# Late modulation of a two-block fp32 network: multiplied and summed by GpSimd along the rows, with eight short TensorE products for the sum over the partitions

## The chip, the cores and the metric

The kernel runs on one core of a Trainium2 chip. The metric is the device time of one launch in microseconds. Engines work side by side and wait for each other by semaphores: TensorE (PE, matrix products; its weight loads are PEld), VectorE (DVE), ScalarE (ACT), GpSimd (POOL) and SyncE (SP), whose queue issues nearly all loads from HBM in the order in which they are written.

## The reference, cut to what matters

Two transformer-like blocks run one behind the other on x of 256 rows by 1024, all in fp32. The first block begins with a modulation of six vectors of 1024 numbers, made from a condition vector c and, for a second input ctx of 256 rows, from c_ctx:

```python
mod_x = silu(c) @ w_mod + b_mod              # w_mod 1024 x 6144, b_mod 6144
mod_c = silu(c_ctx) @ w_mod + b_mod
sh_m, sc_m, gt_m, sh_f, sc_f, gt_f = split(mod_x, 6)
csh_m, csc_m, _, _, _, _ = split(mod_c, 6)   # only these two of c_ctx are used
hx = rms_norm(x, g_pre_mix) * (1 + sc_m) + sh_m
hc = rms_norm(ctx, g_pre_mix) * (1 + csc_m) + csh_m
qa, ka, va, qr, kr, vr, gr = split(h @ w_in)          # for hx and hc
qa = rms_norm(qa, q_norm_g)                  # per head of 64
att, ret = attention(...), retention_both_ways(...)
mix = concat(att, head_group_norm(ret) * silu(gr)) @ w_out
x = x + gt_m * rms_norm(mix, g_post_mix)
hf = rms_norm(x, g_pre_ffn) * (1 + sc_f) + sh_f
x = x + gt_f * rms_norm(swiglu(hf), g_post_ffn)
```

So sh_m and sc_m (the first third of w_mod) are needed before anything can be projected, while gt_m is needed only behind the mix, and sh_f, sc_f, gt_f only for the block's feed-forward part. The second block (two gated feed-forward parts, a chunked linear recurrence, a convolution, cross attention to a memory "mem") isn't touched, but the keys and values of its memory are computed at the very start and in the middle of the first block.

## The kernel before, in words

**Products.** Every fp32 operand is split in a high and a low part, and a product is the sum of three TensorE products: high by high, high by low, low by high (lines 1818 to 1820, `three`). Weights come in 148 units of 1 MB (128 x 2048 numbers). For each, SyncE issues the load into one of three `raw` buffers, ScalarE makes `w_hi` from it (line 641), VectorE makes `w_lo` = raw - w_hi (line 1154), and a raw buffer is free for the load after next but one when `w_lo` is made. TensorE then runs the unit's products, while the other two engines split the next one. Units 0 to 3 are the second block's memory keys (W_K). Units 4 to 14 are `w_in` (W_IN): kr 4, 5; vr 6, 7; ka and va together 8; qa 9, 10; qr 11, 12; gr 13, 14. Units 15 to 18 are `w_out`; then come value units, and from unit 21 on the feed-forward stream. The order of the work on each engine is written out by hand in one function for each engine, with a "bank plan" that says which of TensorE's eight result banks each stage takes and who must have read it before.

**The modulation.** `w_mod` is cut in 24 blocks of 128 x 2048: block m has rows 128·(m mod 8) and columns 2048·(m div 8). `mod_unit(m)` (lines 1907 to 1926) issues four products, one for each 512 columns, with `silu_c` as the stationary operand: 32 columns wide, of which two hold the numbers of c and c_ctx and the others are zeros. The trace records each of the four as two. Their results lie side by side in one bank, `mod_row`. Eight blocks fill one row of 2048 numbers; ScalarE copies it out (`mod_row_out`), four transposes (`mod_T`, line 1933) turn it to columns, and VectorE adds `b_mod` (`mod_columns`, line 1276). Blocks 0 to 7 (sh_m, sc_m) run in the first 32 us between the memory products. Blocks 8 to 23, the late ones, are loaded as 12 "own" loads of 1 MB into two buffers (`memV` and `qrn_qan`, both not needed yet for what they are named after) and 4 in the raw ring between the units. They run on TensorE in six places: 2 behind the transposes of ctx, 3 behind kr, 3 behind unit 6, 3 behind unit 7, 3 behind unit 8 (ka, va) and 2 behind the transposes of krT. `mod_T(1)` stands behind unit 8, `mod_T(2)` behind unit 10.

**What stands around.** At the six places other engines do something for TensorE's next step: behind the ctx transposes ScalarE and VectorE turn them to `hcT_hi` and `hcT_lo` (lines 706, 1204, 1213); behind kr ScalarE copies the four kr banks out (line 719), of which vr takes one; before `states()`, which forms the retention states of ctx, VectorE takes the mean from vr (lines 1336 to 1338). qa is normalised per head: ScalarE copies it to `staged` (line 719), VectorE squares it (line 1394) and sums it (line 1395), ScalarE takes the root (line 813), VectorE the reciprocal (line 1406), and the rotated result is transposed by TensorE ahead of gr (line 1903). The mix's gain is two matrices with a gain on the diagonal, made by VectorE (`gain_diagonal`, line 1435).

**The start.** TensorE first runs six products on whatever lies in memory to raise its clock (line 1989), then transposes mem. ScalarE makes `memT_hi`, VectorE `memT_lo` (line 1240): quarters 0 and 1, then `w_lo` of unit 0, then quarters 2 and 3, then `w_lo` of unit 1. The products of `memT_lo` wait for each quarter.

## Time and profile before

| what | value |
|---|---|
| time, median of 3 runs | 1015.99 us (1015.83 to 1016.72) |
| time of the profiled execution | 1016.42 us |
| its span in the trace | 1014.6 us, so 1.8 us lie outside it |
| granted TensorE clock, mean | 0.998 |
| TensorE busy | 996.7 us, 98% |
| VectorE, ScalarE, GpSimd busy | 585.7, 494.9, 0.2 us |
| read from HBM | 186.61 MB |

The span is the time from the first to the last instruction that the profiler recorded on the core. An engine counts as busy only in instructions that compute. In the chain of waits each step leads back to what released it, so a step there is time that sets the end. In a timeline, the bracket at the end of a row is how long the engine had been idle before it and which instruction ended that.

### The profile page before, as it was taken

Reading aid. Unit: us, or ns where it says so; the run is one execution under the profiler, and the core shown is the slowest. Engines: PE = TensorE matmul, PEld = TensorE weight load, DVE = VectorE, ACT = ScalarE, POOL = GpSimd, SP = SyncE. Lnnn points to the kernel's source line nnn. Section 1 sums busy time; section 2 is a strip of 40 time slices with the busy share of each in tenths; the row PEclk is TensorE's granted clock in tenths of the full one; section 3 lists DMA queues with packets and bytes.
Section 4 is the critical chain, followed back from the end, with each engine's and each line's share of the span. In section 5 each row is a group of like instructions: output and inputs, shape, how many; then the busy total and the mean of one; then the engine's idle time right before and its main releaser. Section 6 shows DMA issues by size and latency. Waiting matters only on the chain.

```text
span 1014.6 us, 13254 instructions
## 1 busy us (share of the span) xinstructions
PE 996.7 (98%) x5168; PEld 811.4 (80%) x5168; DVE 585.7 (58%) x662; ACT 494.9 (49%) x601; POOL 0.2 (0%) x4
## 2 busy tenths in 40 slices
PE   7999999999999999999999999999999999999997
PEld 5877776778888888888888887888888878888885
DVE  5274769667555554565555665557774465555543
ACT  6473337646543443464534534663546554445432
POOL 0000000000000000000000000000000000000000
PEclk9999999999999999999999999999999999999999
DMA  9967653123655545474545465534244245555441
GB/s 371 419 272 295 276 217 125 44 109 129 219 200 176 202 167 207 166 259 171 202 165 186 166 229 177 199 125 140 109 166 166 78 148 190 201 178 201 166 166 42
DMA packets 26686, 188.32 MB, mean 186 GB/s; under 512 B 2960, under 2 KB 3216, under 8 KB 4112
## 3 DMA queue, kind: packets, MB, share of 16 engines
q1 hardware_dynamic: 26064, 185.24, 49.9%
q10 hardware_dynamic: 576, 2.43, 0.6%
...
HBM read 186.61 MB, written 1.05 MB: 185 GB/s over the span
## 4 chain that ended last, share of the span: by engine, by line
PE 93%; DVE 3%; ACT 2%; issue 1%; DMA 0%; ACTq 0%; DVEq 0%
PE bank L1818 24%; PE bank L1820 24%; PE bank L1819 24%; PE bank L2026 2%; PE bank L1862 2%; PE bank L1846 2%; PE bank L1854 2%; PE bank L1924 2%; PE bank L2292 1%; PE bank L1903 1%; PE bank L2390 1%; PE bank L2217 1%; PE bank L2168 1%; PE bank L1989 1%; PE bank L2093 1%
## 5 line engine op out<-in xcount | busy, mean ns | idle before, releaser
L1154 DVE TENSOR_TENSOR w_lo<-raw,w_hi 128x2048 fp32r<-128x2048 f32 x148 | 338.6, 2290 | 265.0 <-ACT w_hi L641 264.9
L641 ACT ACTIVATE w_hi<-raw 128x2048 fp32r<-128x2048 f32 x148 | 283.7, 1918 | 267.2 <-PE bank L1820 217.1
L1818 PE MATMUL bank<-w_hi,hT_hi 128*128 128x512 f32 (+1 forms) x760 | 299.8, 395 | 0.7 <-DVE mod L1276 0.7
L1820 PE MATMUL bank<-w_hi,hT_lo 128*128 128x512 f32 (+1 forms) x760 | 294.9, 388 | 0.0
L1819 PE MATMUL bank<-w_lo,hT_hi 128*128 128x512 f32 (+1 forms) x760 | 294.3, 387 | 0.0
L1818 PEld LDWEIGHTS bank<-w_hi,hT_hi 128*128 128x128 f32 x760 | 142.8, 188 | 33.8 <-issue 4.9
L1820 PEld LDWEIGHTS bank<-w_hi,hT_lo 128*128 128x128 f32 x760 | 142.7, 188 | 29.9
L1819 PEld LDWEIGHTS bank<-w_lo,hT_hi 128*128 128x128 f32 x760 | 142.9, 188 | 27.8 <-issue 0.2
L1818 PE MATMUL bank<-w_hi,gT_hi 128*128 128x512 f32 x264 | 103.4, 392 | 0.0
L1820 PE MATMUL bank<-w_hi,gT_lo 128*128 128x512 f32 x264 | 102.8, 389 | 0.0
L1819 PE MATMUL bank<-w_lo,gT_hi 128*128 128x512 f32 x264 | 102.7, 389 | 0.0
L1820 PEld LDWEIGHTS bank<-w_hi,gT_lo 128*128 128x128 f32 x264 | 49.5, 188 | 10.4
L1819 PEld LDWEIGHTS bank<-w_lo,gT_hi 128*128 128x128 f32 x264 | 49.6, 188 | 10.1
L1818 PEld LDWEIGHTS bank<-w_hi,gT_hi 128*128 128x128 f32 x264 | 49.6, 188 | 10.1
L916 ACT ACTIVATE arena<-bank,rstd 128x256 f32<-128x256 f32 x44 | 18.4, 470 | 63.5 <-PE bank L1820 63.5
L1570 DVE SCALAR_TENSOR_TENSOR arena<-bank,rstd,arena 128x256 f32<-128x256 f32 x44 | 19.2, 478 | 30.8 <-ACT arena L916 30.8
L1576 DVE TENSOR_TENSOR gT_lo<-bank,gT_hi 128x512 f32 (+1 forms) x33 | 22.7, 689 | 3.2
L1846 PE MATMUL bank<-w_hi,hT_hi 128*128 128x512 f32 x88 | 22.3, 395 | 2.2 <-DVE x_res L1558 0.8
L719 ACT ACTIVATE arena<-bank 128x512 f32<-128x512 f32 (+1 forms) x18 | 8.6, 552 | 32.3 <-PE bank L1820 28.8
L916 ACT ACTIVATE arena<-bank 128x256 f32<-128x256 f32 x22 | 7.2, 381 | 31.7 <-PE bank L1820 31.7
L1862 PE MATMUL bank<-w_lo,hT_hi 128*128 128x512 f32 x88 | 22.0, 392 | 0.2 <-DVE w_lo L1154 0.2
L1854 PE MATMUL bank<-w_hi,hT_lo 128*128 128x512 f32 x88 | 22.1, 393 | 0.0
...
## 6 DMA issues: line engine op xcount, KB each, us to landing
raw<-in_weights SPq DMA_DIRECT2D x152, 1024.0 KB, 4.7
arena<-in_first_mods SPq DMA_DIRECT2D x8, 1024.0 KB, 14.2
memV<-in_own_mods SPq DMA_DIRECT2D x6, 1024.0 KB, 4.8
arena<-in_own_mods SPq DMA_DIRECT2D x6, 1024.0 KB, 6.9
...
memV<-in_mem SPq DMA_DIRECT2D x1, 1024.0 KB, 5.9
x_res<-in_x SPq DMA_DIRECT2D x1, 1024.0 KB, 17.6
arena<-in_ctx SPq DMA_DIRECT2D x1, 1024.0 KB, 15.2
```

The source lines that it names most:

```text
L641: act.activation(w_hi[:, v_slot, :], raw[:, u_slot, :], ACT.Copy).then_inc(hi_ready, 1)
L916: act.activation(gate[:, c % 3, tb, :], bank[(c % 3) * 2 + tb][:, 0:256], ACT.Silu, scale=rstd[:, tb:tb + 1] if f else 1.0)\
L1154: ins = dve.tensor_tensor(w_lo[:, v_slot, n], raw[:, u_slot, n], w_hi[:, v_slot, n].bitcast(F32), ALU.subtract)
L1576: dve.tensor_tensor(gT_lo[:, s, :], bank[6][:, :].rearrange("p (a t) -> p a t", t=T), gT_hi[:, s, :].bitcast(F32), ALU.subtract).then_inc( ...
L1818: pe.matmul(out, hi, rhi, start=start, stop=False)
L1819: pe.matmul(out, hi, rlo, start=False, stop=False)
L1820: return pe.matmul(out, lo, rhi, start=False, stop=stop)
L1846: pe.matmul(out[:, :], hT_hi[:, 2 * q + e, tb * P:(tb + 1) * P], weights(w_hi, q, e), start=(first and q == quarters[0] and e == 0), stop= ...
L1854: pe.matmul(out[:, :], hT_lo[:, 2 * q + e, tb * P:(tb + 1) * P], weights(w_hi, q, e), start=False, stop=False)
L1862: ins = pe.matmul(out[:, :], hT_hi[:, 2 * q + e, tb * P:(tb + 1) * P], weights(w_lo, q, e), start=False, stop=(last and q == quarters[1] a ...
L1924: ins = pe.matmul(b[32 * j:32 * j + 32, :], silu_c[:, k, :], w[:, 512 * j:512 * j + 512], start=(k == 0), stop=(k == MOD_K - 1))
L2026: ins = pe.matmul(out[:, :], (lo if x_low else hi)[:, 4 * half + e, tb * P:(tb + 1) * P], w[:, v % RING, e * 512:(e + 1) * 512], start=(st ...
```

## The change

**GpSimd.** The late two thirds of `w_mod` come as 32 steps of 128 x 1024 numbers (512 KB): four parts of 1024 columns by eight blocks of rows. GpSimd multiplies each by its column of silu(c), one number for each partition, and adds it to a sum in `memV` (`mod_sum`). Of 32 steps 4 are a multiplication alone and 28 a multiplication and an addition. Only c is computed, not c_ctx. Steps land in turn in two halves of `qrn_qan`; the load of a step waits until the step two before is summed, and it waits in SyncE's queue, so that the loads of the units behind it wait too. Two to four steps stand behind each of the units 6 to 17.

**TensorE.** `mod_sums(part)` adds a part over the partitions: two products with a stationary operand of ones, 32 columns wide, by 512 columns each. Parts 0 and 1 stand behind units 7 and 11, parts 2 and 3 inside the mix, behind the retention's rows. The sixteen late `mod_unit` are gone. `mod_T(1)` stands behind unit 12, `mod_T(2)` in the mix. Two of the six starting products are gone.

**VectorE and ScalarE.** ScalarE squares qa, straight from the bank, and VectorE only sums. `mod_columns` and the gains move behind, to where the mix needs them. All four quarters of `memT_lo` are made before the first `w_lo`. Normalised qa takes the buffer `ret_p`, since its old place holds the late steps, and the wait for the late modulation's end (`mod_used`) is gone from VectorE.

```diff
-STREAM = [("w", v) for v in range(W_IN + 2)]
-OWN_MODS = {}
-VISITS = {W_IN + 2: 2, W_IN + 3: 3, W_IN + 4: 3, W_IN + 5: 3, W_IN + 6: 3, W_IN + 7: 2}
 W_REG = W_OUT + 2
 while (N_W - W_REG) % RING:
     W_REG += 1
-_m = MOD_K
-for _v in range(W_IN + 2, W_REG):
-    STREAM.append(("w", _v))
-    for _n in range(VISITS.get(_v, 0)):
-        if _n == 2:
-            STREAM.append(("mod", _m))
-        else:
-            OWN_MODS[_m] = (_v, _n)
-        _m += 1
-assert _m == N_MOD
-STREAM += [("w", v) for v in range(W_REG, N_W)]
-HEAD_UNITS = W_REG + N_MOD - MOD_K - len(OWN_MODS)
+STREAM = [("w", v) for v in range(N_W)]
+HEAD_UNITS = W_REG
 RAW_AT = {unit: u for u, unit in enumerate(STREAM)}
-
-
-def mods_behind(v):
-
-    own = [m for m, (at, _) in OWN_MODS.items() if at == v]
-    kind, n = STREAM[RAW_AT[("w", v)] + 1]
-    return own + ([n] if kind == "mod" else [])
+LATE = {v: 2 if W_IN + 2 < v < W_IN + 6 or v == W_OUT else 1 for v in range(W_IN + 2, W_REG)}
+LATE_STEPS = 2 * (N_MOD - MOD_K)
+assert 2 * sum(LATE.values()) >= LATE_STEPS
...
+    plan.streamed(("mod_row", 2), 0)
+    plan.signalled(("modT", 2), 2)
...
+        qan = ret_p
...
-        own_mods = [memV[:].rearrange("p b d -> p (b d)"), qrn_qan]
+        mod_sum = memV[:].rearrange("p b d -> p (b d)")
+        late_mod = [qrn_qan[:, e * 1024:(e + 1) * 1024] for e in range(2)]
...
+            late = [0]
+
+            def late_in(step):
+                if step >= 2:
+                    sp.wait_ge(sem("mod_step"), step - 1)
+                else:
+                    sp.wait_ge(mod_used, MOD_K)
+                sp.dma_start(late_mod[step % 2], io["late_mods"][step]).then_inc(sem(f"late_loaded{step % 2}"), 16)
...
-                kind, v = STREAM[u]
-                if kind == "w" and v in VISITS:
-                    for n, (m, (at, slot)) in enumerate(OWN_MODS.items()):
-                        if at == v:
-                            sp.wait_ge(mod_used, mods_behind(v)[0])
-                            sp.dma_start(own_mods[slot], io["own_mods"][n]).then_inc(sem(f"own_mod_loaded{slot}"), 16)
+                for _ in range(2 * LATE.get(u, 0)):
+                    if late[0] < LATE_STEPS:
+                        late_in(late[0])
+                        late[0] += 1
...
+        @block.gpsimd
+        def _(pool):
+            pool.wait_ge(sem("silu_c"), 1)
+            filled(pool, ("memT", 3))
+            for step in range(LATE_STEPS):
+                part, k = step // MOD_K, step % MOD_K
+                total = mod_sum[:, part % 2 * 1024:(part % 2 + 1) * 1024]
+                pool.wait_ge(sem(f"late_loaded{step % 2}"), 16 * (step // 2 + 1))
+                if k == 0:
+                    if part >= 2:
+                        pool.wait_ge(sem("mod_summed"), part - 1)
+                    pool.tensor_scalar(total, late_mod[step % 2], silu_c[:, k, 0:1], None, ALU.mult).then_inc(sem("mod_step"), 1)
+                else:
+                    pool.tensor_scalar(late_mod[step % 2], late_mod[step % 2], silu_c[:, k, 0:1], None, ALU.mult)\
+                        .then_inc(sem("mod_scaled"), 1)
+                    pool.wait_ge(sem("mod_scaled"), step - part)
+                    pool.wait_ge(sem("mod_step"), step)
+                    pool.tensor_tensor(total, late_mod[step % 2], total, ALU.add).then_inc(sem("mod_step"), 1)
...
-            mod_row_out(1)
...
-            mod_row_out(2)
             used(W_IN + 6)
             act.wait_ge(sem("kr_done"), 1)
+            act.wait_ge(sem("rope_done"), 4)
             for tb in range(TB):
+                act.activation((rope_a, rope_b)[tb], bank_of(("qa", tb))[:, :], ACT.Square).then_inc(sem("qa_squared"), 1)
                 copy_out(("qa", tb), staged[:, tb, :])
...
             act.activation(kaT[:, :], b[:, :], ACT.Copy).then_inc(read_sem(("kaT", 0)), 1)
+            mod_row_out(1)
...
+            mod_row_out(2)
...
-            split_T("memT", col("mem_norm"), hi=memT_hi, lo=memT_lo, qs=[0, 1])
-            low_to(W_K + 1)
-            split_T("memT", col("mem_norm"), hi=memT_hi, lo=memT_lo, qs=[2, 3])
+            split_T("memT", col("mem_norm"), hi=memT_hi, lo=memT_lo)
             low_to(W_K + 2)
...
+            for tb in range(TB):
+                dve.wait_ge(sem("qa_squared"), tb + 1)
+                ins = dve.reduce_sum(head_ss[:, tb * 8:tb * 8 + 8], heads((rope_a, rope_b)[tb]), AX.X)
+            ins.then_inc(sem("qa_ss"), 1)
             read_out(dve, ("qa", 1))
-            for tb in range(TB):
-                chain(dve.tensor_tensor(rope_a, staged[:, tb, :], staged[:, tb, :], ALU.mult))
-                ins = dve.reduce_sum(head_ss[:, tb * 8:tb * 8 + 8], heads(rope_a), AX.X)
-                if tb == 0:
-                    chain(ins)
-            ins.then_inc(sem("qa_ss"), 1)
             low_to(W_IN + 10)
-            mod_columns(2)
-            dve.tensor_tensor(gain_col[:, 0, :], mod[:, 16:24, 0], col("g_post_mix"), ALU.mult)
-            dve.tensor_scalar(a_ffn[:, :], mod[:, 32:40, 0], 1.0, None, ALU.add)
-            chain(dve.tensor_tensor(gain_col[:, 1, :], mod[:, 40:48, 0], col("g_post_ffn"), ALU.mult))
-            dve.tensor_tensor(a_ffn[:, :], a_ffn[:, :], col("g_pre_ffn"), ALU.mult).then_inc(sem("ffn_cols"), 1)
             dve.wait_ge(sem("qa_rms"), 1)
             chain(dve.reciprocal(head_rstd[:, :], head_rms[:, :]))
             for tb in range(TB):
                 ins = dve.tensor_tensor(heads(staged[:, tb, :]), heads(staged[:, tb, :]),
                                         heads_bc(head_rstd[:, tb * 8:tb * 8 + 8], HEADS, HD), ALU.mult)
             chain(ins)
-            dve.wait_ge(mod_used, N_MOD)
...
+            mod_columns(1)
+            dve.tensor_tensor(gain_col[:, 0, :], mod[:, 16:24, 0], col("g_post_mix"), ALU.mult).then_inc(sem("gain_col"), 1)
...
+            dve.wait_ge(sem("gain_col"), 1)
+            dve.wait_ge(sem("mod_step"), LATE_STEPS)
+            gain_diagonal(0)
...
-            for g in range(2):
-                gain_diagonal(g)
+            mod_columns(2)
+            dve.tensor_scalar(a_ffn[:, :], mod[:, 32:40, 0], 1.0, None, ALU.add)
+            chain(dve.tensor_tensor(gain_col[:, 1, :], mod[:, 40:48, 0], col("g_post_ffn"), ALU.mult))
+            dve.tensor_tensor(a_ffn[:, :], a_ffn[:, :], col("g_pre_ffn"), ALU.mult).then_inc(sem("ffn_cols"), 1)
+            gain_diagonal(1)
...
+            def mod_sums(part):
+
+                g = 1 + part // 2
+                pe.wait_ge(sem("mod_step"), MOD_K * (part + 1))
+                b = free(pe, ("mod_row", g)) if part % 2 == 0 else bank_of(("mod_row", g))
+                for e in range(2):
+                    j = part % 2 * 2 + e
+                    ins = pe.matmul(b[32 * j:32 * j + 32, :], ones[:, 0:32], mod_sum[:, 512 * j:512 * j + 512], start=True, stop=True)
+                ins.then_inc(sem("mod_summed"), 1)
...
-            for _ in range(6):
+            for _ in range(4):
...
-            for m in mods_behind(W_IN + 2):
-                mod_unit(m)
...
-                    if j < 6:
-                        for m in mods_behind(W_IN + j + 2):
-                            mod_unit(m)
-                    if j == 6:
-                        mod_T(2)
+                    if j in (3, 7):
+                        mod_sums(j // 4)
+                    if j == 8:
+                        mod_T(1)
...
+            def rows_and_sums():
+                retained_rows()
+                for part in (2, 3):
+                    mod_sums(part)
+
+            mix_out(0, 0, {1: rows_and_sums})
+            mix_out(0, 1, {0: lambda: mod_T(2)})
```

The first place in the order is TensorE's, from the last transposes of ctx to the first product of unit 6; a row here is a group of like instructions. Before:

```order
L1941 MATMUL bank<-fixed,arena 128x128 x12
L1924 MATMUL bank<-memV,silu_c 32x512 x4
L1924 MATMUL bank<-arena,silu_c 32x512 x4
L2026 MATMUL bank<-w_hi,hcT_hi 128x512 x8
L1941 MATMUL bank<-fixed,arena 128x128 x4
L2026 MATMUL bank<-w_hi,hcT_lo 128x512 x8
L2026 MATMUL bank<-w_lo,hcT_hi 128x512 x8
L2026 MATMUL bank<-w_hi,hcT_hi 128x512 x8
L2026 MATMUL bank<-w_hi,hcT_lo 128x512 x8
L2026 MATMUL bank<-w_lo,hcT_hi 128x512 x8
L1924 MATMUL bank<-memV,silu_c 32x512 x4
L1924 MATMUL bank<-arena,silu_c 32x512 x4
```

After:

```order
L1949 MATMUL bank<-fixed,arena 128x128 x12
L2034 MATMUL bank<-w_hi,hcT_hi 128x512 x8
L1949 MATMUL bank<-fixed,arena 128x128 x4
L2034 MATMUL bank<-w_hi,hcT_lo 128x512 x8
L2034 MATMUL bank<-w_lo,hcT_hi 128x512 x8
L2034 MATMUL bank<-w_hi,hcT_hi 128x512 x8
L2034 MATMUL bank<-w_hi,hcT_lo 128x512 x8
L2034 MATMUL bank<-w_lo,hcT_hi 128x512 x8
```

The two blocks ahead of the products of `hcT_hi` (line 2026 before, 2034 after) and the ones behind them are gone: these products now follow the transposes at once, and unit 6 the products of kr.

The second place is SyncE's queue of loads, from unit 6 on. Before:

```order
L574 DMA raw<-in_weights 128x2048
L609 DMA memV<-in_own_mods 128x2048
L609 DMA arena<-in_own_mods 128x2048
L611 DMA arena<-in_const 128x772
L574 DMA raw<-in_weights 128x2048
L609 DMA memV<-in_own_mods 128x2048
L609 DMA arena<-in_own_mods 128x2048
L574 DMA raw<-in_weights 128x2048 x2
L609 DMA memV<-in_own_mods 128x2048
```

After:

```order
L555 DMA raw<-in_weights 128x2048
L569 DMA arena<-in_late_mods 128x1024 x2
L599 DMA arena<-in_const 128x772
L555 DMA raw<-in_weights 128x2048
L569 DMA arena<-in_late_mods 128x1024 x4
L555 DMA raw<-in_weights 128x2048
L569 DMA arena<-in_late_mods 128x1024 x4
L555 DMA raw<-in_weights 128x2048
L569 DMA arena<-in_late_mods 128x1024 x4
```

Where one or two blocks of 1 MB stood behind a unit's load, there are two or four of 512 KB, each behind a wait for GpSimd, which the load of the next unit stands behind as well.

The third place is VectorE's queue where qa is normalised, between the making of `w_lo` of two units. Before:

```order
L1154 TENSOR_TENSOR w_lo<-raw,w_hi 128x2048
L1394 TENSOR_TENSOR arena<-arena 128x512
L1395 TENSOR_REDUCE head_ss<-arena 128x8
L1394 TENSOR_TENSOR arena<-arena 128x512
L1395 TENSOR_REDUCE head_ss<-arena 128x8
L1154 TENSOR_TENSOR w_lo<-raw,w_hi 128x2048
L1276 TENSOR_TENSOR mod<-bank,cols 128x32
L1401 TENSOR_TENSOR gain_col<-mod,cols 128x8
L1402 TENSOR_SCALAR a_ffn<-mod 128x8
L1403 TENSOR_TENSOR gain_col<-mod,cols 128x8
L1404 TENSOR_TENSOR a_ffn<-a_ffn,cols 128x8
```

After:

```order
L1165 TENSOR_TENSOR w_lo<-raw,w_hi 128x2048
L1402 TENSOR_REDUCE head_ss<-arena 128x8 x2
L1165 TENSOR_TENSOR w_lo<-raw,w_hi 128x2048
L1407 RECIPROCAL head_rstd<-head_rms 128x16
L1409 TENSOR_TENSOR arena<-arena,head_rstd 128x512 x2
```

The two squarings of 128 x 512 (line 1394) left the queue, and so did the five small instructions of the last modulation row between `w_lo` and the reciprocal (line 1406 before, 1407 after).

## Rows read from the trace of the kernel before

**Rows 1.** The page: busy time by engine.

```profile
PE 996.7 (98%) x5168; PEld 811.4 (80%) x5168; DVE 585.7 (58%) x662; ACT 494.9 (49%) x601; POOL 0.2 (0%) x4
```

**Rows 2.** Waits of TensorE, 12 to 225 us: in total, times, longest.

```profile
PE bank L1903 <- ACT arena L719: 1.2, 1, 1.2
PE bank L1967 <- DVE memT_lo L1240: 0.8, 1, 0.8
PE bank L1818 <- DVE mod L1276: 0.7, 1, 0.7
```

**Rows 3.** Windows with line 1924 alone: length, TensorE busy, weight loads busy, clock, DMA.

```profile
70.00:80.00 10.00, 2.78 (x24) 0.68 (x24) 1.00 0.64 251
...
sum 52.00, PE 14.98 PEld 3.54; mean PE 2.50 PEld 0.59
```

**Rows 4.** Chain that ended last, 60 to 78 us: start us, us, what.

```profile
62.05 1.85 PE bank L1924 x16
...
75.51 2.71 PE bank L1924 x24
```

**Rows 5.** Timeline of TensorE at five places: start us, us, line, operation, idle before.

```profile
33.45 0.36 PE L1818 MATMUL bank<-memT_hi,w_hi 128*128 128x256 f32 x1
...
117.44 0.60 PE L1933 MATMUL bank<-fixed,mod_row 128*128 128x128 f32 x4
...
121.46 0.50 PE L1818 MATMUL bank<-w_hi,hT_hi 128*128 128x512 f32 x1 [0.71 <-DVE mod L1276]
...
127.17 1.03 PE L2058 MATMUL bank<-arena 128*64 128x64 f32 x27
...
211.37 3.76 PE L2263 MATMUL bank<-arena,fixed 128*128 128x512 f32 x8
```

**Rows 6.** Timeline of ScalarE at six places.

```profile
24.41 1.15 ACT L697 ACTIVATE xn<-x_res,rstd 128x1024 f32<-128x1024 f32 x1 [0.23 <-DVE rstd L1180]
...
61.22 1.93 ACT L706 ACTIVATE hcT_hi<-bank,mod,a_mix 128x256 fp32r<-128x256 f32 x4 [1.44 <-PE bank L1941]
...
75.55 2.06 ACT L719 ACTIVATE arena<-bank 128x512 f32<-128x512 f32 x4 [3.46 <-PE bank L2026]
...
105.14 1.94 ACT L641 ACTIVATE w_hi<-raw 128x2048 fp32r<-128x2048 f32 x1
...
138.84 1.09 ACT L719 ACTIVATE arena<-bank 128x512 f32<-128x512 f32 x2 [4.90 <-PE bank L1820]
...
160.74 1.92 ACT L641 ACTIVATE w_hi<-raw 128x2048 fp32r<-128x2048 f32 x1
```

**Rows 7.** Timeline of VectorE at six places.

```profile
24.41 0.76 DVE L1184 TENSOR_SCALAR xn<-x_res,rstd 128x1024 f32<-128x1024 f32 x1
...
30.57 2.29 DVE L1154 TENSOR_TENSOR w_lo<-raw,w_hi 128x2048 fp32r<-128x2048 f32 x1 [5.40 <-ACT w_hi L641]
...
62.27 1.91 DVE L1204 TENSOR_SCALAR shifted_T<-bank,a_mix,mod 128x256 f32<-128x256 f32 x4 [3.10 <-ACT hcT_hi L706]
...
121.22 0.18 DVE L1276 TENSOR_TENSOR mod<-bank,cols 128x32 f32<-128x32 f32 x1
...
139.96 0.69 DVE L1394 TENSOR_TENSOR arena<-arena 128x512 f32<-128x512 f32 x1 [5.16 <-ACT arena L719]
...
145.59 0.24 DVE L1406 RECIPROCAL head_rstd<-head_rms 128x16 f32<-128x16 f32 x1
```

**Rows 8.** Lines of 205 to 215 us: busy us, mean ns of one.

```profile
L1435 DVE TENSOR_TENSOR arena<-fixed,gain_col 128x1024 f32<-128x1024 f32 x2 | 2.4, 1216 | 0.0
```

**Rows 9.** Windows: length, then PE, PEld, DVE, ACT, POOL busy, clock, DMA share, GB/s.

```profile
10.00:50.00 40.00, 39.17 (x301) 30.40 (x300) 16.81 (x21) 19.45 (x26) 0.00 (x0) 1.00 1.01 422
50.00:200.00 150.00, 147.80 (x1066) 110.06 (x1065) 106.78 (x200) 82.26 (x137) 0.00 (x0) 1.00 0.53 206
```

**Rows 10.** The queue of the loads, its issue near 46 us: start us, us.

```profile
46.27 0.33 SPq L609 DMA_DIRECT2D memV<-in_own_mods  x1
```

**Rows 11.** The page, DMA issues: KB each, us from issue to landing.

```profile
raw<-in_weights SPq DMA_DIRECT2D x152, 1024.0 KB, 4.7
```

More of the change, by code:

```diff
@@ L428, in two_blocks_kernel @@
         qrn_qan = carve(at, UNIT)
-        qrn = carve(at, TB, 512); at += 1024
-        qan = carve(at, TB, 512); at += 1024
+        gain_diag = [carve(at + g * 1024, 1024) for g in range(2)]; at += 1024
+        at += 1024
         k_fb = carve(at, 2, TB, 512)
@@ L1363, in _ @@
                 centre_values(tile)
-            mod_columns(1)
             read_out(dve, ("kava", 3))
@@ L1909, in mod_unit @@
                 g, k = m // MOD_K, m % MOD_K
-                if g == 0:
-                    pe.wait_ge(sem(f"mod_loaded{m}"), 16)
-                    w = first_mod[m % len(first_mod)]
-                elif m in OWN_MODS:
-                    slot = OWN_MODS[m][1]
-                    loads = sum(s == slot and n <= m for n, (_, s) in OWN_MODS.items())
-                    pe.wait_ge(sem(f"own_mod_loaded{slot}"), 16 * loads)
-                    w = own_mods[slot]
-                else:
-                    u = RAW_AT[("mod", m)]
-                    pe.wait_ge(raw_ready[u % RING], 16 * (u // RING + 1))
-                    w = raw[:, u % RING, :]
+                pe.wait_ge(sem(f"mod_loaded{m}"), 16)
+                w = first_mod[m % len(first_mod)]
                 b = free(pe, ("mod_row", g)) if k == 0 else bank_of(("mod_row", g))
@@ L2606, in lay_out @@
         "weights": np.stack([units[kind][n] for kind, n in STREAM]),
-        "first_mods": np.stack(mods[:MOD_K]), "own_mods": np.stack([mods[m] for m in OWN_MODS]),
+        "first_mods": np.stack(mods[:MOD_K]), "late_mods": np.stack([f("w_mod")[0][k * P:(k + 1) * P, c:c + 1024] for c in range(MOD_K * 256, N_MOD * 256, 1024)
+                               for k in range(MOD_K)]),
         "cols": np.concatenate([small[name] for name in COLS], axis=1),
```

22 lines of the change are left out of this document (6 added, 16 removed).

## Prediction

> **What bounds the kernel now.** I read the busy times first: TensorE works 996.7 us of a span of 1014.6, VectorE 585.7, ScalarE 494.9, GpSimd nothing [rows 1]. So the time is TensorE's work plus some 18 us in which it stands. The list of its waits up to 225 us comes next, since the change ends there: 1.2 us at the transposes of qa, 0.8 us at the low parts of mem, 0.7 us for the bank that VectorE's `mod_columns` reads [rows 2]. They are small, so what counts is work taken from TensorE, and whether other engines still keep up with it once it is gone. Then the windows with line 1924 alone: the sixteen late blocks stand in six places, and together they are busy 14.98 us [rows 3]. Last I looked at the chain there: it runs through them, 1.85 us for two blocks and 2.71 us for three [rows 4], so they lie on the path that sets the end.
>
> **TensorE: what goes.** Two places of two blocks and four of three: 2 x 1.85 + 4 x 2.71 = 14.5 us off (the 14.98 count each stretch's last modelled end as well). The wait of 0.71 us ahead of 121.46 [rows 5] goes with the move of the modulation's bank: 0.7 us off. `mod_T(1)` takes 117.44 to 117.96, 0.5 us [rows 5]. It moves behind unit 12, into the 1.2 us that TensorE waits there for ScalarE: 0.5 us off. `mod_T(2)` costs as much in the mix as it did: 0.
>
> **TensorE: what comes.** Four `mod_sums` of two products, side by side in column groups like the four of a block. A block is 2.71 / 3 = 0.90 us. If the four of a block run beside each other, two take as long as four; if they share a width, half. A full-width fp32 product by 512 columns takes 3.76 / 4 = 0.94 us (four products, recorded as eight) [rows 5], 1.9 us for two in sequence. So a part costs between 0.45 and 1.9 us; I take 0.9, the row of the same shape, thus 3.6 us in all (1.8 to 7.5).
>
> **The start.** Two starting products less and the low parts made without a `w_lo` between them: the wait of 0.8 us [rows 2] should go. But the memory products can't run ahead of the data. VectorE's `w_lo` that ends at 30.57 + 2.29 = 32.86 is used at 33.45 [rows 5, 7], 0.6 us later, and the loads have the queue full from 10 to 50 us (share 1.01, 422 GB/s) [rows 9], so `w_hi`, which that `w_lo` waits for, can't be earlier. I take 0.6 us off, between 0 and 0.9.
>
> **Covers that go.** A removed block also hid something. (1) Behind the ctx transposes: ScalarE's `hcT_hi` starts at 61.22, before TensorE is done with them at 62.05, and the first of its four pieces takes 1.93 / 4 = 0.5 us. TensorE needs it at once now, where it had 1.85 us: 0.5 us on (0 to 1.0). VectorE's `hcT_lo` has the high products and four transposes ahead of it, so nothing there. (2) Behind kr ScalarE copies four banks from 75.55 on, 2.06 / 4 = 0.5 us each, and vr takes one of them [rows 6]. Three blocks covered that. Now TensorE waits for the first copy and its semaphore: 0.7 us on (0.5 to 1.2). (3) `states()` needs the four centred vr. VectorE is done with them at 121.22 [rows 7], and TensorE reaches `states()` at 127.17 [rows 5], 5.95 us later. Counted from the end of unit 7, from where both go on, VectorE keeps its time and TensorE loses 2 x 2.71 for the six blocks, 0.52 for `mod_T(1)` and 0.71 for the wait, and gains one sum of 0.9: 5.75 us. That leaves a margin of 0.2 us, and a copy or a `w_lo` that comes in another order uses it up: 0.4 us on (0 to 1.2).
>
> **qa.** Squaring by ScalarE is 2 x 0.55 us there and 2 x 0.7 us off VectorE. The rms waited for the second sum. VectorE squares and sums from 139.96 to 142.8 and comes to the reciprocal only at 145.59 [rows 7], behind a `w_lo` and five small instructions. These go and the `w_lo` starts with ScalarE's later `w_hi`: 138.84 + 4 x 0.55 + 1.92 gives 142.96, and 2.29 more 145.25, 0.3 us earlier than 145.59. What follows is the wait of 1.2 us, which ends on ScalarE's copy of qr, not on qa [rows 2]. So the squares are worth 0 (up to 0.3 off). The two gain matrices, 1.2 us each [rows 8], and the columns go to where TensorE has a unit of gr ahead of it: 0 (0 to 1.0 on).
>
> **Sum.** -14.5 + 3.6 - 0.7 - 0.5 - 0.6 + 0.5 + 0.7 + 0.4 = -11.1 us. The profiled execution took 1016.42 us (1014.6 of span, 1.8 around it): 1005.3. It stood 0.4 us above the median of the three runs; for such a median I say 1005.1, between that and the sum less 0.4. With every term at its better end I get -14.5 + 1.8 - 1.2 - 0.9 + 0.5 - 0.3 = -14.6, with each at its worse -14.5 + 7.5 - 1.2 + 1.0 + 1.2 + 1.2 + 1.0 = -3.8; the terms don't err together, so this case's own range is 1002.5 to 1010.
>
> **GpSimd's step.** All this holds only if GpSimd keeps pace, and no row shows it computing. Bound it by others on 128 x 1024: a multiplication takes VectorE 0.76 us and ScalarE 1.15 us [rows 6, 7]; an addition of two operands takes VectorE 1.22 us [rows 8], and 2.29 us for twice the elements [rows 7], which I take as the slow end. A step is 2.0 to 3.4 us. I take 3.4, the slower end, since no row speaks for GpSimd being as fast as VectorE. The Trainium skill, "GPSIMD Engine Reference", section 3.1 "Elementwise — side-by-side cycle accounting", gives 4497 ns on GpSimd for an fp32 addition of 2048 elements against 2293 ns on VectorE; the row agrees on VectorE's part, and half of 4497 plus 1.15 would be a step of 3.4 too. The first own load was issued at 46.27 [rows 10], a unit takes 4.7 us to land [rows 11], so step 0 begins near 51. SyncE's queue stands behind GpSimd: the load of unit 10 waits until step 11 is done. `w_hi` of unit 10 starts at 105.14 [rows 6], now some 6.7 us earlier, and the load must be issued 4.7 us ahead: by 93.7. Ten full steps and two short ones (1.15 us) fit into the 42.7 us between if a step takes under 4.0 us. Unit 16's `w_hi` is at 160.74 [rows 6], now 10.7 us earlier, its load due by 145.3 and behind step 25: 22 full steps and four short ones, again 4.0 us. At 3.4 us both gates are open and the cost is 0. Bytes are the same, and the loads' share in 50 to 200 us is 0.53 [rows 9].
>
> **Rival: the two engines shut each other out.** GpSimd and VectorE work on the same memory, and it may be that they can't both be in it. VectorE is busy 106.8 of the 150 us from 50 to 200 [rows 9], which shrink to 139. GpSimd brings 28 x 2.0 + 4 x 0.76 = 59 us at the fast end and 28 x 3.4 + 4 x 1.15 = 100 us at the slow one. In sequence these are 166 or 207 us, 27 or 68 us more than there is: 1005 plus these, 1032 to 1073. I put the case at 1045, since some of VectorE's work reads result banks alone. It decides once the overlap that is lost exceeds the 32 us that VectorE stands idle. For it: `w_lo` of each unit stands on the path from load to product. Against it: nothing in the trace, where GpSimd never runs. The Trainium skill says it outright ("SBUF — State Buffer", "SBUF: two separate sides"): the two share a pair of ports that is locked for a whole instruction when VectorE has two operands in SBUF, or runs in its two-port mode, and GpSimd reads SBUF; `w_lo` and the rotations are such instructions, and no run here shows it yet. By that rule the time would be this rival's.
>
> **Rival: a step is simply too slow.** Each 0.1 us over 4.0 adds 2.2 us by unit 16. At 4.4 us the gain is nearly gone (1014), at 4.6 it is a loss (1018). It is on the slower side from 4.5 us on, where the 11 us are used up. For it: a landing time of 4.7 us, if 512 KB took as long, would make a period of (3.4 + 4.7) / 2 = 4.05, since each buffer's load waits for its step. Against it: both bounds of the step are below, and half a load should land sooner.
>
> **Rival: the sums wait.** If GpSimd is late for a part, TensorE stands in `mod_sums`. The last part stands in the mix, behind all of the projections. Step 31 would end at 51 + 28 x 3.4 + 4 x 1.15 = 151 us, before even unit 16's `w_hi`, so this can only come as a part of the slow step, and has no chance of its own.
>
> **How the numbers follow.** My forecast 0.46. The shut-out 0.38, all slower. The slow step 0.14: 0.04 faster, 0.06 same, 0.04 slower. The rest 0.02 slower for what I don't see. A measurement of this kernel can tell some 0.2%, 2 us. So faster 0.5, same 0.06, slower 0.44. The range must reach into the shut-out case until 2 in 10 are left out: 1003 to 1060.
>
> **What would show it.** Right: TensorE has none of the sixteen blocks, four sums of 0.9 us, waits of half a microsecond near 61 and 73 us, `w_lo` still 2290 ns in the mean, `w_hi` never waiting for a load from 60 to 160 us, and GpSimd done by 155 us. Wrong: `w_lo` or the rotations take longer than before, or VectorE stands with its operands ready while GpSimd runs (shut-out); `w_hi` released by loads that SyncE issued late (slow step).

## The result, and the profile after

The changed kernel takes 1076.21 us (median of 4 runs, 1075.12 to 1077.8), the one before 1016.32 beside it: a ratio of 1.0593, 95% interval 1.058 to 1.0605. The forecast was 1005.1 with a range up to 1060. The time lies above the range, and on the side of both rivals.

The page of the changed kernel: busy times, slices of TensorE, of GpSimd and of the granted clock, and the chain that ended last by engine.

```profile
PE 997.2 (93%) x5052; PEld 817.2 (76%) x5052; DVE 638.9 (59%) x660; ACT 496.2 (46%) x603; POOL 184.7 (17%) x64
...
PE   7997708779999999999999999999999999999997
...
POOL 0099999990000000000000000000000000000000
PEclk9999758899999999999999999999999999999999
...
PE 75%; POOL 14%; DVE 4%; DMA 3%; issue 2%; ACT 1%; SPq 1%; POOLq 0%; DVEq 0%; ACTq 0%
```

TensorE is busy 997.2 us in 5052 instructions, where it was 996.7 in 5168 [rows 1], but the span grew by 61 us to 1075.4. The loss lies in slices four to nine of 40 (26.9 us each; the sixth has nothing at all), and GpSimd works in three to nine. GpSimd is 14% of the chain, TensorE 75%.

Its costliest groups: `w_lo`, `w_hi`, and GpSimd's multiplication (line 636) and addition (line 640).

```profile
L1165 DVE TENSOR_TENSOR w_lo<-raw,w_hi 128x2048 fp32r<-128x2048 f32 x148 | 342.9, 2319 | 283.3 <-ACT w_hi L648 283.1
L648 ACT ACTIVATE w_hi<-raw 128x2048 fp32r<-128x2048 f32 x148 | 283.7, 1918 | 307.1 <-PE bank L1828 217.4
...
L636 POOL TENSOR_SCALAR arena<-arena,silu_c 128x1024 f32<-128x1024 f32 x28 | 95.1, 3396 | 1.0 <-DMA arena<-in_late_mods 1.0
L640 POOL TENSOR_TENSOR memV<-arena,memV 128x1024 f32<-128x1024 f32 x28 | 75.2, 2687 | 2.3
```

A full step is 3.4 + 2.7 = 6.1 us where the prediction had 3.4 in all. `w_hi` waited 307 us in all (267 before). `w_lo` has a mean of 2319 ns for 2290, over all 148 units.

TensorE's longest waits by line from 10 to 300 us, in the form of [rows 2]:

```profile
PE bank L2066 <- issue: 25.6, 1, 25.6
PE bank L1826 <- DVE w_lo L1165: 9.3, 2, 9.0
PE bank L1933 <- POOL memV L640: 6.2, 1, 6.2
```

Before, the longest was 1.2 us [rows 2]. Now it stands 25.6 us at the retention states (line 2066), 9.0 us ahead of unit 8's products, 6.2 us in the first `mod_sums` (line 1933). Two of these go back to loads that came late. ScalarE's `w_hi` of units 9 and 10, and VectorE's queue from unit 10's `w_lo` to the last centring of vr, for which the states wait:

```profile
110.11 1.91 ACT L648 ACTIVATE w_hi<-raw 128x2048 fp32r<-128x2048 f32 x1 [23.16 <-DMA raw<-in_weights]
...
132.87 1.92 ACT L648 ACTIVATE w_hi<-raw 128x2048 fp32r<-128x2048 f32 x1 [16.50 <-DMA raw<-in_weights]
```

```profile
134.83 3.30 DVE L1165 TENSOR_TENSOR w_lo<-raw,w_hi 128x2048 fp32r<-128x2048 f32 x1 [19.88 <-ACT w_hi L648]
...
158.71 1.57 DVE L1347 TENSOR_TENSOR arena<-arena,value_mean 128x512 f32<-128x512 f32 x1
```

The 9.0 us are put down to a `w_lo`, but that one (112.05) is unit 9's, and unit 8's was made at 93.9. By the program unit 8 also needs a bank that ScalarE's copy of vr frees; the copy starts at 114.36, in ScalarE's queue behind unit 9's `w_hi`. In the run with four fills (below) the profile names this copy for the same wait, 8.2 us. The 25.6 us can be taken apart with the run in which GpSimd is narrowed (below). There VectorE starts unit 10's `w_lo` 14.2 us before TensorE is ready for the states, here 0.1 us after: 14.3 us from the late start. From this `w_lo` to the last centring VectorE takes 25.4 us here and 15.1 there: 10.4 us from longer instructions. The wait of that run, 1.0 us, is the rest.

Now both engines in one stretch. First GpSimd's timeline, then VectorE's:

```profile
52.90 5.53 POOL L634 TENSOR_SCALAR memV<-arena,silu_c 128x1024 f32<-128x1024 f32 x1 [52.47 <-DMA arena<-in_late_mods]
...
91.15 5.40 POOL L636 TENSOR_SCALAR arena<-arena,silu_c 128x1024 f32<-128x1024 f32 x1
...
101.92 2.34 POOL L640 TENSOR_TENSOR memV<-arena,memV 128x1024 f32<-128x1024 f32 x1
104.23 2.84 POOL L634 TENSOR_SCALAR memV<-arena,silu_c 128x1024 f32<-128x1024 f32 x1
...
110.45 2.34 POOL L640 TENSOR_TENSOR memV<-arena,memV 128x1024 f32<-128x1024 f32 x1
112.78 4.88 POOL L636 TENSOR_SCALAR arena<-arena,silu_c 128x1024 f32<-128x1024 f32 x1
...
238.38 2.35 POOL L640 TENSOR_TENSOR memV<-arena,memV 128x1024 f32<-128x1024 f32 x1
```

```profile
87.03 4.69 DVE L1352 TENSOR_TENSOR arena<-arena,ctx_decay 128x512 f32<-128x512 f32 x4
91.64 2.28 DVE L1165 TENSOR_TENSOR w_lo<-raw,w_hi 128x2048 fp32r<-128x2048 f32 x1
112.05 2.90 DVE L1165 TENSOR_TENSOR w_lo<-raw,w_hi 128x2048 fp32r<-128x2048 f32 x1 [18.12 <-ACT w_hi L648]
```

Lay them side by side. Undisturbed, a multiplication takes 2.84 us (104.23) and an addition 2.34 (101.92). VectorE's `w_lo` starts at 91.64 and ends at 93.92, at its old 2.28 us. GpSimd's multiplication is issued at 91.15, when VectorE is in the last of four multiplications of two SBUF operands (line 1352, until 91.7), and ends at 96.55, 2.6 us behind the `w_lo` that follows them: it did next to nothing until then. At 112.05 it is the other way round: GpSimd's addition is at work until 112.8, and `w_lo` takes 2.90 us, the 0.7 us until that end and its own 2.2. The next multiplication, at 112.78, takes 4.88, and is over 2.7 us behind this `w_lo`. In each of these places the one that comes second does nothing until the other is done; so both engines have longer rows.

Windows of the changed kernel, columns as in [rows 9]:

```profile
115.20:120.40 5.20, 5.20 (x24) 5.20 (x25) 0.00 (x0) 1.17 (x3) 5.12 (x3) 0.50 0.02 7
...
140.00:160.00 20.00, 0.00 (x0) 0.00 (x0) 19.66 (x30) 4.25 (x3) 19.23 (x8) 0.50 0.41 156
160.00:180.00 20.00, 16.46 (x143) 14.16 (x144) 19.69 (x25) 7.05 (x9) 19.75 (x7) 0.79 0.56 207
```

From 140 to 160 us TensorE does nothing, and its granted clock is 0.50, the lower level of 1.2 GHz; in the next 20 us, at work again, it has 0.79 in the mean. It is the same behind the waits of 6.2 and 9.0 us: from 115.2 to 120.4 us TensorE is busy throughout and the clock is 0.50; a product of 128 x 256 comes each 0.21 us there, and each 0.12 us from 120.5 on. So a long wait costs once more behind itself. The size of it: with GpSimd narrowed (below) the same 5052 instructions keep TensorE busy 983.0 us, here 997.2, so 14 us. Behind 262 us here and behind 190 us there the busy time is the same, 803.2 us of 813, so the whole loss lies before.

### The profile page after: what moved, and what is told of

Its sections match the earlier page's. It is cut to its first block, busy times and chain, and to the rows that moved or that the text cites. A ratio compares the mean times of both kernels' runs of the same rounds, so it can differ in the third digit from the quotient of the medians.

```text
span 1075.4 us, 13083 instructions
## 1 busy us (share of the span) xinstructions
PE 997.2 (93%) x5052; PEld 817.2 (76%) x5052; DVE 638.9 (59%) x660; ACT 496.2 (46%) x603; POOL 184.7 (17%) x64
## 4 chain that ended last, share of the span: by engine, by line
PE 75%; POOL 14%; DVE 4%; DMA 3%; issue 2%; ACT 1%; SPq 1%; POOLq 0%; DVEq 0%; ACTq 0%
PE bank L1826 20%; PE bank L1828 20%; PE bank L1827 20%; POOL arena L636 7%; POOL memV L640 6%; DMA raw<-in_weights 3%; PE bank L1870 2%; PE bank L1854 2%; PE bank L1862 2%; POOL memV L634 1%; PE bank L2298 1%; PE bank L2396 1%; DVE arena L1432 1%; PE bank L1911 1%; PE bank L2510 1%
## 5 line engine op out<-in xcount | busy, mean ns | idle before, releaser
L1165 DVE TENSOR_TENSOR w_lo<-raw,w_hi 128x2048 fp32r<-128x2048 f32 x148 | 342.9, 2319 | 283.3 <-ACT w_hi L648 283.1
L1826 PE MATMUL bank<-w_hi,hT_hi 128*128 128x512 f32 (+1 forms) x760 | 303.3, 399 | 13.0 <-DVE w_lo L1165 9.0
L1827 PE MATMUL bank<-w_lo,hT_hi 128*128 128x512 f32 (+1 forms) x760 | 297.8, 392 | 0.0
L1826 PEld LDWEIGHTS bank<-w_hi,hT_hi 128*128 128x128 f32 x760 | 145.3, 191 | 46.3 <-issue 18.7
L1828 PEld LDWEIGHTS bank<-w_hi,hT_lo 128*128 128x128 f32 x760 | 145.2, 191 | 30.1
L636 POOL TENSOR_SCALAR arena<-arena,silu_c 128x1024 f32<-128x1024 f32 x28 | 95.1, 3396 | 1.0 <-DMA arena<-in_late_mods 1.0
L640 POOL TENSOR_TENSOR memV<-arena,memV 128x1024 f32<-128x1024 f32 x28 | 75.2, 2687 | 2.3
L2066 PE MATMUL bank<-arena 128*64 128x64 f32 x64 | 3.7, 316 | 25.6 <-issue 25.6
L634 POOL TENSOR_SCALAR memV<-arena,silu_c 128x1024 f32<-128x1024 f32 x4 | 14.8, 3697 | 52.5 <-DMA arena<-in_late_mods 52.5
```

Source lines behind the costliest of these rows:

```text
L634: pool.tensor_scalar(total, late_mod[step % 2], silu_c[:, k, 0:1], None, ALU.mult).then_inc(sem("mod_step"), 1)
L636: pool.tensor_scalar(late_mod[step % 2], late_mod[step % 2], silu_c[:, k, 0:1], None, ALU.mult)\
L640: pool.tensor_tensor(total, late_mod[step % 2], total, ALU.add).then_inc(sem("mod_step"), 1)
L1165: ins = dve.tensor_tensor(w_lo[:, v_slot, n], raw[:, u_slot, n], w_hi[:, v_slot, n].bitcast(F32), ALU.subtract)
L1826: pe.matmul(out, hi, rhi, start=start, stop=False)
L1827: pe.matmul(out, hi, rlo, start=False, stop=False)
```

## Experiments

**GpSimd narrowed.** Is the sum for the other engines right? This kernel leaves out most of the late modulation's arithmetic.

```diff
-pool.tensor_scalar(late_mod[s], late_mod[s], silu_c[:, k, 0:1], None, ALU.mult)
-pool.tensor_tensor(total, late_mod[s], total, ALU.add)
+pool.tensor_scalar(late_mod[s][:, 0:16], late_mod[s][:, 0:16], silu_c[:, k, 0:1], None, ALU.mult)
+pool.tensor_tensor(total[:, 0:16], late_mod[s][:, 0:16], total[:, 0:16], ALU.add)
```

> The changed kernel with GpSimd's 28 multiplications and 28 additions cut to 16 of their 1024 columns; the four first steps and all loads, waits and TensorE work stay. The sums behind the modulation are mostly left out. If the predicted sum for TensorE was right and only GpSimd's price was wrong: 1003 to 1008 us, no wait for a load at w_hi, w_lo back at 2290 ns. If the new order on the other engines itself costs time (bare waits at the ctx transposes, kr, states, the later modulation columns): 1012 or more.

Measured: 1005.10 us (1005.03 to 1005.19); ratio 0.9891 (0.9876 to 0.9906). Busy times, TensorE's waits, and the four sums (line 1933 alone, columns as in [rows 3]):

```profile
PE 983.0 (98%) x5052; PEld 807.5 (80%) x5052; DVE 586.9 (58%) x660; ACT 495.6 (49%) x603; POOL 49.0 (5%) x64
```

```profile
PE bank L2066 <- issue: 1.0, 1, 1.0
PE bank L1826 <- ACT arena L726: 0.9, 1, 0.9
PE bank L1911 <- ACT arena L726: 0.8, 1, 0.8
...
PE bank L2034 <- ACT hcT_hi L713: 0.3, 1, 0.3
```

```profile
50.00:200.00 150.00, 3.17 (x16) 0.45 (x16) 1.00 0.57 210
```

The bare waits are there, each 1 us at most, and the sums take 3.17 us where the blocks took 14.98 [rows 3]. So nothing but the width of GpSimd's instructions separates 1005 from 1076: 71 us. GpSimd is still busy 49.0 us in this run, of which four full multiplications are 15.1.

**GpSimd at full width, nobody waits.** Twenty steps, and only the shut-out is left. TensorE's sums read another tensor, so the late modulation is left out.

```diff
-for step in range(LATE_STEPS):
-    pool.wait_ge(sem(f"late_loaded{step % 2}"), 16 * (step // 2 + 1))
+for step in range(20):                       # loads of steps 0 and 1 alone
...
-    pe.wait_ge(sem("mod_step"), MOD_K * (part + 1))
-    ... mod_sum[:, 512 * j:512 * j + 512]
+    if part == 3:
+        pe.wait_ge(sem("mod_step"), 20)
+    ... memKT (flat)[:, 512 * j:512 * j + 512]
```

> The changed kernel in which GpSimd runs 20 full steps, multiplication and addition at their full width, but nobody waits for one: only the first two late loads are made, SyncE's queue has no wait for GpSimd, TensorE's sums read another tensor; the only wait left is in the mix, for step 20. It leaves out the late modulation. If the two engines shut each other out and that made most of the 60 us: 1030 or more, with VectorE's rotations and centring 1.3 to 2 times as long and TensorE waiting for VectorE. If the closed gate for the loads made most of it: 1005 to 1015, though single VectorE instructions are still longer, and a step near 5.3 us.

Measured: 1035.14 us (1034.52 to 1036.12), 30.0 above the narrow run. The step was done at 174.5 us, before the mix, so the last wait cost nothing. Of the 30.0 us, 8.4 are TensorE's longer busy time (991.4 us against 983.0) at a granted clock of 0.986 in the mean; the others are waits. The longest of them, most for VectorE (at the first the profile names nobody; it is the states' wait for VectorE's centring, as above):

```profile
PE bank L2067 <- issue: 9.3, 1, 9.3
PE bank L1911 <- DVE mod L1287: 6.7, 1, 6.7
PE bank L1826 <- issue: 5.2, 1, 5.2
```

VectorE by form, first in the narrow run (50 to 200 us), then here (50 to 175 us); the mean ns stand behind the busy us:

```profile
L1165 DVE TENSOR_TENSOR w_lo<-raw,w_hi 128x2048 fp32r<-128x2048 f32 x13 | 29.7, 2286 | 14.9 <-ACT w_hi L648 14.8
...
L1345 DVE TENSOR_REDUCE value_mean<-arena 128x8 f32<-128x512 f32 x4 | 2.7, 677 | 0.0
...
L1346 DVE TENSOR_SCALAR value_mean<-value_mean 128x8 f32<-128x8 f32 x4 | 0.8, 194 | 0.1
```

```profile
L1165 DVE TENSOR_TENSOR w_lo<-raw,w_hi 128x2048 fp32r<-128x2048 f32 x11 | 30.8, 2808 | 5.2 <-ACT w_hi L648 5.1
...
L1215 DVE TENSOR_SCALAR shifted_T<-bank,a_mix,mod 128x256 f32<-128x256 f32 x16 | 7.6, 534 | 3.1 <-ACT hcT_hi L713 3.1
...
L1346 DVE TENSOR_SCALAR value_mean<-value_mean 128x8 f32<-128x8 f32 x4 | 4.4, 1106 | 0.1
...
L1345 DVE TENSOR_REDUCE value_mean<-arena 128x8 f32<-128x512 f32 x4 | 2.7, 673 | 0.0
```

Here is which forms suffer. `w_lo`, with two operands in SBUF, takes 2808 ns for 2286. A `tensor_scalar` of 128 x 8 from SBUF takes 1106 ns for 194. A reduction from SBUF over 512 numbers keeps its 673 ns (677), and a `tensor_scalar` that reads a result bank takes 534 ns in both. The Trainium skill states this rule ("SBUF — State Buffer", "SBUF: two separate sides"): the pair of ports is locked for a whole instruction, for VectorE with two SBUF operands while GpSimd reads SBUF, or in its two-port mode. The trace agrees in these four forms.

**Fills in place of arithmetic.** The narrow run, with fills behind each addition, which take GpSimd's time but read nothing; the late modulation is left out here too.

```diff
+for n in range(4):                           # 3 and 2 in the other two runs
+    pool.memset(late_mod[step % 2][:, 0:1024], 0.0)   # each waits for the last
```

> The changed kernel with GpSimd's multiplications and additions cut to 16 columns, as in the narrow run, and four fills of 128 x 1024 with zeros behind each addition, so that a step takes about 5 us but reads next to nothing; all waits stay. The late modulation is left out. If GpSimd's bare pace and the closed gate alone cost time: unit 10's load waits until 51 + 10 x 5.3 + 2 x 2.8 = 110 us instead of 94, and the last sum until 211 instead of 189: 1020 to 1030 us, with VectorE's instructions at their old lengths. If all of the 71 us lost come from pace, 1076. If fills shut VectorE out as well, over 1040 with longer w_lo.

Measured: 1051.57 us (1048.55 to 1051.82). GpSimd's fills and VectorE's `w_lo` from 50 to 212 us:

```profile
L644 POOL MEMSET arena<- 128x1024 f32 x112 | 107.5, 960 | 6.5
...
L1174 DVE TENSOR_TENSOR w_lo<-raw,w_hi 128x2048 fp32r<-128x2048 f32 x12 | 27.5, 2289 | 38.9 <-ACT w_hi L657 38.9
```

`w_lo` is back at 2289 ns, so this is pace in the main, and it costs 46.5 us, where I expected 15 to 25. It isn't pace alone: besides four full multiplications and the narrow instructions, the fills themselves hold VectorE's `tensor_scalar` up. At 127.92 us one of 128 x 8 takes 0.91 us, while GpSimd is in nothing but fills from 127.85 to 131.8, and it ends with the first of them; the sixteen of 128 x 512 that scale the attention (line 1441) take 768 ns for 484 in the mean.

> The run with four fills behind each addition, with three: a step of about 4.0 us instead of 5.0. By the prediction's gates (4.0 us a step is the limit) it costs little: 1006 to 1010. If pace costs per step from lower on, as 46 us over 32 steps of 5.0 might mean 1.4 us a step: a third less than the run with four fills, near 1030.

Measured: 1029.45 us (1026.31 to 1030.35). The rival was right: steps 1 to 7 took 4.2 us each, and the prediction's 2.2 us for each 0.1 over 4.0 would give 5 us, not 24. ScalarE's `w_hi` of units 9 and 16 in it, and TensorE's two long waits:

```profile
92.91 1.92 ACT L657 ACTIVATE w_hi<-raw 128x2048 fp32r<-128x2048 f32 x1 [15.13 <-DMA raw<-in_weights]
...
171.59 1.91 ACT L657 ACTIVATE w_hi<-raw 128x2048 fp32r<-128x2048 f32 x1 [12.04 <-DMA raw<-in_weights]
```

```profile
PE bank L2075 <- issue: 11.3, 1, 11.3
PE bank L2227 <- DVE arena L1441: 9.3, 1, 9.3
```

Unit 9's is the first late one. It stands idle 15 us, of which 8.2 are there in the narrow run too, for TensorE; it starts 7.2 us later than there. Its load stands behind step 7, and the prediction had looked at the gates of units 10 and 16 only. Unit 16's gate is closed as well. In the complete kernel, with a step of 6.1 us, even unit 8's load is late, behind step 3: its `w_hi` waits 7.7 us for it.

> The same with two fills: a step of about 3.0 us. Unit 9's load, which the prediction's gates left out, stands behind step 7: with a first step of 5.5 us from 52 us on and a need at 81 us, the limit is (81 - 57.5) / 7 = 3.3 us a step. If that is the first gate to close, this run costs nothing: 1005 to 1007. If pace costs at any step, 8 us less than three fills per fill taken away: near 1012.

Measured: 1015.18 us (1012.82 to 1016.17), 10 above the narrow run. I had expected 0 below a limit of 3.3 us. The gate was the right one, the step was not 3.0 us: GpSimd's narrow multiplications and additions wait for VectorE as the wide ones do (0.33 us alone, up to 2.8 here), and steps 1 to 7 took 58.8 to 87.0 us, 4.0 each. Unit 9's load was issued at 87.4 instead of 77.3, and its `w_hi` started at 92.8 instead of 85.7. So a step of 4.0 us in that stretch is already over the limit; where exactly the cost starts these runs don't show. With three fills unit 9's load is issued at 87.5, the same, so the 14 us between the two runs come from later gates: at the states TensorE waits 7.5 us with two fills and 11.3 with three, and the 9.3 us at line 2227 are there with three alone, where unit 16's `w_hi` waits 12.0 us for its load (0.8 with two).

**Late loads on GpSimd's own queue.** The complete kernel, without the gate for the units.

```diff
-for _ in range(2 * LATE.get(u, 0)):          # SyncE, behind each unit's load
-    late_in(late[0]); late[0] += 1
+if u == W_IN + 2: late_in(0); late_in(1)
...
+pool.dma_start(late_mod[step % 2], io["late_mods"][step + 2])   # GpSimd, behind each step
```

> The changed kernel, complete, but late loads from the third on are issued by GpSimd on its own queue when a step is done, so no unit's load waits for GpSimd. TensorE still waits for the sums. If the closed gate in SyncE's queue makes a good part of the 71 us: 1050 to 1062, no wait for a load at w_hi, and a wait of TensorE at its last sums. If it is only the last sum and the shut-out that count, because the work must be done in any case: 1070 to 1080.

Measured: 1078.4 us (1077.54 to 1079.18), 2 more than the change itself. The gate is open: `w_hi` waits 256 us over the whole, less than the 267 before (page, line 653 of this kernel).

```profile
L653 ACT ACTIVATE w_hi<-raw 128x2048 fp32r<-128x2048 f32 x148 | 283.7, 1918 | 255.9 <-PE bank L1833 225.0
```

But TensorE now waits in the sums, which the prediction had as a part of the slow step:

```profile
PE bank L1938 <- POOL memV L642: 50.8, 3, 25.9
```

50.8 us in three waits, for GpSimd's addition. So opening the gate alone doesn't bring the time back. The gate is where lateness showed first; the work itself, 32 steps of 5.2 us and more from 52 us on, ends after TensorE needs it. GpSimd's last addition ended at 240.7 us in the changed kernel and, with 0.6 us for each load that it issues, at 260.7 here. A queue whose issue costs GpSimd nothing wasn't tried, so how much the open gate would gain by itself stays open; the 20 us that GpSimd is later may hide a gain.

**Half the work on GpSimd.** TensorE keeps the blocks 8 to 15 (the middle third of `w_mod`), GpSimd does 16 steps.

```diff
-LATE_STEPS = 2 * (N_MOD - MOD_K)
+LATE_STEPS = 2 * MOD_K                       # steps 16 to 31 of the change
+for m in (...): mod_unit(m)                  # 8 at ctx, 9 and 10 behind kr, 11 to 13 behind units 6 to 8, 14 and 15 behind 9
```

> The same split of the work as in the version with fused steps, TensorE with 8 late blocks, but GpSimd does the 16 steps in two operations as in the change, at most two loads behind a unit. GpSimd would be done by 52 + 16 x 5.8 = 145 us, long before the last sums near 190, so its pace should cost nothing. If the shut-out costs 1.5 us a step, as in the free run (30 us for 20 steps): 1011 + 24 = 1035 (1028 to 1040). If only the pace counts in complete kernels: 1011 to 1015.

Measured: 1029.91 us (1029.59 to 1030.71), ratio 1.0134 (1.0119 to 1.015). GpSimd was done at 175 us, later than I said, since its loads came two or fewer behind a unit, but before the sums. TensorE's waits are VectorE's again:

```profile
PE bank L1923 <- DVE arena L1280: 7.4, 1, 7.4
PE bank L1923 <- DVE mod L1298: 5.7, 1, 5.7
```

**No GpSimd.** VectorE does these 16 steps in one instruction each, where it stood.

```diff
+dve.scalar_tensor_tensor(out=total, in0=late_mod[step % 2], scalar=silu_c[:, k, 0:1], in1=total,
+                         op0=ALU.mult, op1=ALU.add).then_inc(sem("mod_step"), 1)
...
+late_steps(2)      # ahead of the ctx transposes; behind w_lo of unit 7; ahead of 8; (4) ahead of 10;
+                   # behind the sums of qa; behind w_lo of unit 16; behind 17
```

> A version without GpSimd: VectorE itself multiplies and adds in one instruction, 16 steps of 128 x 1024 for the last third of w_mod, placed where it waited for w_hi; TensorE keeps 8 of the 16 late blocks (the middle third). Start, squares, late columns as in the change. TensorE: -14.5 + 7.2 + 2 x 0.9 - 0.7 - 0.5 - 0.6 = -7.3 us, so 1009 if the steps of 1.22 us are hidden in VectorE's gaps; if those at 129, 154 and 184 us are not, or VectorE waits for their loads, 1011 to 1015.

Measured: 1011.42 us (1010.72 to 1013.52), ratio 0.996 (0.9946 to 0.9974): faster than before, 2.4 us over the sum. A step of VectorE, and the two waits of TensorE that stand out:

```profile
L1174 DVE SCALAR_TENSOR_TENSOR memV<-arena,silu_c,memV 128x1024 f32<-128x1024 f32 x14 | 17.9, 1282 | 1.3 <-DMA arena<-in_late_mods 0.5
```

```profile
PE bank L1930 <- DVE arena L1279: 1.3, 1, 1.3
PE bank L2127 <- ACT arena L836: 1.1, 1, 1.1
```

Then four of the steps at other places:

```diff
 low_to(W_IN + 9)
+late_steps(2)                                # ahead of the sums of qa, no longer behind them
...
 low_to(W_OUT + 2)
-late_steps(2)
+# one ahead of the last normalise(p), one behind retention_probs(0)
```

> The version with VectorE's fused steps, with four of its sixteen steps at other places: two ahead of the sums of qa, where VectorE stood 2.3 us idle, one ahead of the last normalisation and one between the retention's products, where it stood 1.7 and 1.1 us. If these four made the waits of TensorE of 1.3 us at the transposes and 1.1 us at the attention, both go: 1009.0 (1008.5 to 1010). If the waits have other causes: 1011.4 again.

Measured: 1009.09 us (1008.55 to 1009.62), ratio 0.9931 (0.9918 to 0.9945). Both waits are gone:

```profile
PE bank L1932 <- ACT arena L717: 0.8, 1, 0.8
PE bank L2004 <- DVE w_lo L1159: 0.6, 1, 0.6
```

Against half the work on GpSimd, 1029.91, this is 20.8 us less, 1.3 us for each of the 16 steps (18.5 us, 1.2 for each, with the steps where they stood first). The version leaves no part of the computation out and beats both kernels, by 7.1 and 67 us.

**The small parts alone.** On the kernel before, the start (four products, low parts first; the edit shown), and the start with ScalarE's squares as in the change:

```diff
-for _ in range(6):
+for _ in range(4):
...
-split_T("memT", ..., qs=[0, 1]); low_to(W_K + 1); split_T("memT", ..., qs=[2, 3])
+split_T("memT", ...)
```

> The kernel before with the change at the start alone: 0.6 us off, between 0 and 0.9, so 1015.1 to 1016.0. Together with the run with the squares it gives the squares by themselves.

> The kernel before with two small parts of the change alone: low parts of mem first and four starting products, and the squares of qa by ScalarE. Predicted terms: 0.6 us off for the start (0 to 0.9), 0 for the squares (up to 0.3 off): 1015.4 against 1016.0. A rival: ScalarE is the later engine at qa and the squares cost up to 1.1 us there: 1016.5.

Measured: 1015.75 (ratio 0.9995, 0.9986 to 1.0005) and 1015.61 (0.9995, 0.9986 to 1.0004), against 1016.18 with 21 runs. Both are consistent with 0.6 us off and 0 for the squares, and neither can be told from no change.

## Why the prediction was wrong

**The sum for TensorE, VectorE and ScalarE was right.** It gave 1005.1, and with GpSimd's instructions narrowed the kernel takes 1005.10. A part of such closeness is luck, since the terms were known to 0.3 us or so. Sums: 3.6 said, 3.2 measured. Copy of kr: 0.7 said, 0.9 measured. States: 0.4 said, 1.0 (line 2066), of which 0.8 are GpSimd's: eight instructions of VectorE ahead of the centring (line 1363) take 2.97 us for 2.19 before, beside one of the four full multiplications that are left. Transposes of ctx: 0.5 said, 0.3 + 0.4, the 0.4 for VectorE's `hcT_lo`, where the prediction had nothing. Of the wait of 1.2 us at qa 0.8 is left (line 1911 for ScalarE's copy), where I had 0.5 off.

**The step that failed first is "A step is 2.0 to 3.4 us".** A multiplication alone takes GpSimd 2.84 us. I had bounded it by 1.15, ScalarE's row, as if a third engine had to lie between the two that I saw. No row of before showed GpSimd computing, and rows of other engines bound nothing there. The addition, at 2.34, was near the 2.29 that I took as its slow end. The figure of the Trainium skill's "GPSIMD Engine Reference", section 3.1, halved, an estimate, had given 2.25 for it. The bare step is 5.2 us, and by the prediction's own slow-step rival, over 4.5 us, the kernel is on the slower side: the rival had the mechanism and 0.14 of the chance, because its condition was held to be out of bounds.

**The gate was a second fault.** I let step 0 take 1.15 us from 51 on; it took 5.5 from 52.9 and ended at 58.4. That alone takes the limit for unit 10 from 4.0 to (93.7 - 58.4 - 2.8) / 10 = 3.2 us. I also left out unit 9, whose load stands behind step 7 and is needed by 81 us; with the start that I had assumed, its limit would be (81 - 52.2) / 7 = 4.1, no tighter than the others, and with the real one it is 3.2. So the start was the fault more than the unit left out. The price per step was too low as well: with a step of 5.0 the run with four fills costs 46.5 us, where "2.2 us for each 0.1 over 4.0" gives 22. Some of it is the fills' hold on VectorE, and 9.5 us are TensorE's longer busy time (992.5 us against 983.0), which no term had.

**The shut-out is real, and was put at the right size.** Twenty steps that nobody waits for cost 30 us, in proportion (an estimate) 48 for 32; the rival had 27 to 68 for all. It had 0.38 of the chance, and its range reached 1073.

**What was wrong in the frame:** I treated the two rivals as exclusive. Both came true, and they feed each other: each GpSimd step waits for VectorE (5.2 us bare, 5.9 from 52.9 to 240.7 us over 32), and VectorE, whose `w_lo` and rotations are late, holds TensorE. Pace is at most 46.5 us, the shut-out 30 for 20 steps, and in the kernel of 32 steps both together cost 71. How the 71 us divide is not a number that the runs give; only for the longest wait do the rows give it, 14.3 us for the late start and 10.4 for longer instructions, and even this late start has GpSimd's waits for VectorE in it. A range to hold both together had to reach beyond 1075.

What I gave for signs held: `w_lo` longer than before, `w_hi` released by late loads, for each cause its own. GpSimd was done at 240.7 us, not by 155.
